# A fused block of three layers on one core: the first layer multiplies its raw input, and the RMS roots are applied behind the products

## The chip, the cores and the metric

One NeuronCore of a Trainium2 chip runs the whole program. The metric is device time in microseconds (us) from start to end of one execution; the median of three runs of the kernel before is 909.2 us (908.95 to 911.43). All data is float32; the big products run as three fp32r products of split operands. A difference of less than about 0.3% (2.7 us) can't be told from no change.

## The reference, cut to what matters

Three residual layers in a row on 256 tokens of width 1024. The change is in the first ("even") layer and in two places at the start of the second ("odd") one.

```python
def rms_norm(x, g):
    xf = x.astype(jnp.float32)
    y = xf * lax.rsqrt(jnp.mean(xf * xf, axis=-1, keepdims=True) + EPS)
    return (y * g.astype(jnp.float32)).astype(x.dtype)

def even_layer(h, mem, layer, norm_g, w_in, w_out, a_qn, a_kn, a_lam, a_on,
               b_cw, b_cb, x_qn, x_kn, mem_g, w_mem_kv):
    u = rms_norm(h, norm_g)
    proj = u @ w_in                      # 1024 -> 7168 columns
    aq, ak, av, az, bh, bc, bb, bz, xq, xz = jnp.split(proj, cuts, axis=-1)
    ya = differential_attention(aq, ak, av, a_qn, a_kn, a_lam, a_on, lam_init)   # 8 heads "A"
    yb = short_gated_conv(bh, bc, bb, b_cw, b_cb)        # bb * conv3(bc * bh)
    yx = memory_cross_attention(xq, mem, mem_g, w_mem_kv, x_qn, x_kn)            # 4 heads "X"
    y = jnp.concatenate([ya * jax.nn.silu(az), yb * jax.nn.silu(bz), yx * jax.nn.silu(xz)], axis=-1)
    return h + y @ w_out
```

The root of the first norm, 1/sqrt(mean(x^2)+eps), is one number per token. Because the product is linear, it can be multiplied onto a token's row of `proj` instead of onto `x`; where `proj` is normed again (q and k), it cancels but for the eps.

## The kernel before

**Tiling.** A weight matrix is read in *panels* of 512 columns, and a panel in four *subs* of 2 x 128 rows (512 KB each). For every sub SP loads `raw` (six slots), ScalarE (ACT) casts it into `whi`, VectorE (DVE) computes `wlo = raw - whi`, and TensorE (PE) multiplies `whi`, `wlo`, `whi` with the high, high and low part of the input. A slot of `raw` is free when `wlo` was made of it. In orientation "tok" the result has tokens on partitions (12 matmuls of 512 columns in a sub), in "col" it has features on partitions (24 matmuls of 256 columns). Results collect in two PSUM accumulators `acc` used in turn.

**Order.** `make_plan` writes one list of steps; each engine runs its share of it in that order. `pl.at(pos, ...)` hangs a step behind the sub of number `pos`. The `split` step (cast and `wlo`) of a sub is placed three subs ahead of its product (`LEAD = 3`), so DVE and ACT may run at most that far ahead, and everything else that they do stands between the splits. Subs 0 to 63 are the first layer's input panels, with the weights for the memory in between; subs 64 to 79 are `e_w_out`.

**Start.** SP loads `x` in two halves of 128 tokens, ACT squares them, GpSimd (POOL) takes the root, DVE scales the rows (L2652), PE turns them by 16 transposes (L1394, L1410), ACT and DVE take them out of PSUM as `xhi` and `xlo` in `xx` (L1766, L2658). Gains and other vectors come as rows and are turned by PE into `cols`.

**Heads.** Each head has steps qkT (transposes), scores, PT, pv; an A head also has oT: its output is scaled by its norm (L2377), turned, multiplied by gate and gain into `ytmp` (DVE L2385), cast into `yhi` (ACT L1927) and subtracted for `ylo` (DVE L2340). The panels 3072 and 3584 are the gates of the A heads, 6656 the gate of the X heads, 4096, 4608, 5120, 5632 the four inputs h, c, b, z of the convolution.

**Second layer.** The forget gate's logarithm (`forget_log`, `forget_sum`) and the first X head (head 12) stand at subs 92 to 98.

Between all this DVE also sums the modulation of the third layer out of `w_mod` (`macc`, L2403), eight halves a chunk, whose loads use the same `raw` slots.

## Time and profile before

| what | value |
|---|---|
| median of 3 runs | 909.2 us (908.95 to 911.43) |
| the profiled execution, its own time | 909.54 us |
| its span, first to last instruction | 907.7 us |
| PE busy, DVE busy, ACT busy | 887.4, 694.6, 509.6 us |
| mean granted TensorE clock | 0.998 |

How to read it: PE's matmuls are pipelined, so "busy" covers small gaps. What one costs is the distance between the starts of two in a row, and a gap shows as a larger distance and in the bracket behind a row ("[0.73 <-DVE wlo L2137]": idle 0.73 us before, released by that). An "x4" row is several merged, with the time that they span. Start times are us from the span's start. PEclk is the granted clock of a stretch (1.00 is 2.4 GHz, 0.50 is 1.2 GHz). The chain of waits is the work that ended last, followed back: each row is a piece of it.

### The profile page before, as it was taken

The page shows a single profiled execution, that of the slowest core. Times are in us where ns is not written, and L with a number is a line of the kernel's source. Part 1 is how long each engine was busy: PE and PEld are TensorE (multiplying, and loading weights), DVE is VectorE, ACT ScalarE, POOL GpSimd, SP SyncE. Part 2 cuts the span into 40 slices and gives each one's busy share as a digit, 9 for nine tenths or more (in the row PEclk, how much of TensorE's full clock was granted, in tenths as well). Part 3 has the DMA queues.
Part 4 walks back from the last instruction along what each step waited for, and adds up shares of the span by engine and source line. Part 5 has one row for each costly group of instructions (what it writes and reads, how often), then busy time and mean ns, then how long its engine had stood idle before and what let it go on. Part 6 is the DMA issues. An engine that isn't in the chain of part 4 may idle for free.

```text
span 907.7 us, 13941 instructions
## 1 busy us (share of the span) xinstructions
PE 887.4 (98%) x5136; PEld 748.0 (82%) x5136; DVE 694.6 (77%) x1094; ACT 509.6 (56%) x902; POOL 85.7 (9%) x82
## 2 busy tenths in 40 slices
PE   7999999999999999999999999999999999999997
PEld 5888878999788788988889887877787688888885
DVE  6789989879777568788898765878757779877553
ACT  6567564664445555555576646546645755555441
POOL 0302121100001101102111000100001100010000
PEclk9999999999999999999999999999999999999999
DMA  9754644736665755768767764453223468875541
GB/s 329 270 193 158 236 136 145 260 136 217 223 237 158 235 185 193 248 227 280 267 210 237 262 209 151 127 187 93 93 94 114 153 201 272 281 224 192 193 157 46
DMA packets 103125, 177.71 MB, mean 196 GB/s; under 512 B 7118, under 2 KB 32147, under 8 KB 102931
## 3 DMA queue, kind: packets, MB, share of 16 engines
q1 hardware_dynamic: 99856, 167.27, 55.1%
q0 software_dynamic: 2896, 9.42, 3.0%
q8 instruction: 42, 0.69, 0.3%
q14 instruction: 25, 0.20, 0.1%
q10 hardware_dynamic: 306, 0.14, 0.1%
HBM read 175.71 MB, written 1.07 MB: 195 GB/s over the span
## 4 chain that ended last, share of the span: by engine, by line
PE 79%; DVE 12%; ACT 4%; issue 3%; DMA 1%; POOL 1%; ACTq 0%; DVEq 0%; POOLq 0%
PE acc L1295 15%; PE acc L1297 14%; PE acc L1296 14%; PE acc L1357 9%; PE acc L1358 4%; DVE wlo L2137 4%; PE acc L1306 4%; PE acc L1307 4%; PE acc L1308 4%; ACT whi L1700 1%; DVE macc L2403 1%; PE tp L1452 1%; PE spsum L1436 1%; PE opsum L1575 1%; PE tp L1420 1%
## 5 line engine op out<-in xcount | busy, mean ns | idle before, releaser
L2137 DVE TENSOR_TENSOR wlo<-raw,whi 128x1024 fp32r<-128x1024 f32 (+2 forms) x274 | 324.6, 1193 | 101.0 <-ACT whi L1700 100.5
L1700 ACT CAST whi<-raw 128x1024 fp32r<-128x1024 f32 (+2 forms) x274 | 278.2, 1026 | 106.0 <-PE acc L1297 63.1
L1295 PE MATMUL acc<-whi,xx 128*128 128x512 f32 (+1 forms) x352 | 143.4, 408 | 1.9 <-DVE xx L2661 1.0
L1297 PE MATMUL acc<-whi,xx 128*128 128x512 f32 (+1 forms) x352 | 136.4, 388 | 0.0
L1296 PE MATMUL acc<-wlo,xx 128*128 128x512 f32 (+1 forms) x352 | 135.9, 386 | 0.0
L1357 PE MATMUL acc<-xx,whi 128*128 128x512 f32 x352 | 123.1, 394 | 0.9 <-DVE xx L2646 0.8
L1306 PE MATMUL acc<-xx,whi 128*128 128x256 f32 x384 | 112.7, 293 | 0.0
L1308 PE MATMUL acc<-xx,whi 128*128 128x256 f32 x384 | 108.6, 283 | 0.0
L1307 PE MATMUL acc<-xx,wlo 128*128 128x256 f32 x384 | 108.5, 283 | 0.0
L1358 PE MATMUL acc<-xx,wlo 128*128 128x256 f32 x352 | 98.2, 279 | 0.0
L2734 POOL TENSOR_TENSOR small<-small,half_neg 128x8 f32<-128x8 f32 (+4 forms) x30 | 50.5, 1683 | 444.8 <-DVE small L2098 269.5
L1295 PE MATMUL acc<-whi,yhi 128*128 128x512 f32 x224 | 89.2, 398 | 0.8 <-DVE wlo L2137 0.7
L1297 PE MATMUL acc<-whi,ylo 128*128 128x512 f32 x224 | 87.3, 390 | 0.0
L1296 PE MATMUL acc<-wlo,yhi 128*128 128x512 f32 x224 | 87.3, 390 | 0.0
L2403 DVE SCALAR_TENSOR_TENSOR macc<-raw,scol,macc 128x512 f32<-128x512 f32 x112 | 82.2, 755 | 0.0
L1295 PEld LDWEIGHTS acc<-whi,xx 128*128 128x128 f32 x352 | 66.5, 189 | 17.0 <-issue 5.4
L1357 PEld LDWEIGHTS acc<-xx,whi 128*128 128x128 f32 x352 | 65.9, 187 | 17.4 <-DVE xx L2646 1.4
L1297 PEld LDWEIGHTS acc<-whi,xx 128*128 128x128 f32 x352 | 66.3, 188 | 14.3
L1296 PEld LDWEIGHTS acc<-wlo,xx 128*128 128x128 f32 x352 | 66.7, 189 | 11.9
L1306 PEld LDWEIGHTS acc<-xx,whi 128*128 128x128 f32 x384 | 73.5, 191 | 1.4 <-issue 1.1
L1307 PEld LDWEIGHTS acc<-xx,wlo 128*128 128x128 f32 x384 | 73.5, 191 | 0.3
L1308 PEld LDWEIGHTS acc<-xx,whi 128*128 128x128 f32 x384 | 73.4, 191 | 0.0
(409 smaller groups left out, 1399.8 us busy)
## 6 DMA issues: line engine op xcount, KB each, us to landing
raw<-in_e_w_in SPq DMA_DIRECT2D x56, 512.0 KB, 5.6
raw<-in_o_w_in SPq DMA_DIRECT2D x56, 512.0 KB, 5.6
raw<-in_w_mod SPq DMA_DIRECT2D x48, 512.0 KB, 4.3
raw<-in_w_ffn_in SPq DMA_DIRECT2D x44, 512.0 KB, 4.9
raw<-in_w_in SPq DMA_DIRECT2D x28, 512.0 KB, 3.9
raw<-in_w_ffn_out SPq DMA_DIRECT2D x22, 512.0 KB, 4.2
raw<-in_e_w_out SPq DMA_DIRECT2D x16, 512.0 KB, 6.3
raw<-in_o_w_out SPq DMA_DIRECT2D x16, 512.0 KB, 4.9
```

Source lines behind the costliest of these rows:

```text
L1295: mm(o, hi, whi[:, slot, k, 0:pan.ncols], start=a, stop=False)
L1296: mm(o, hi, wlo[:, slot, k, 0:pan.ncols], start=False, stop=False)
L1297: last = mm(o, lo, whi[:, slot, k, 0:pan.ncols], start=False, stop=z)
L1306: mm(o, wh, hi, start=a, stop=False, skip_group_check=True)
L1307: mm(o, wl, hi, start=False, stop=False, skip_group_check=True)
L1308: return mm(o, wh, lo, start=False, stop=z, skip_group_check=True)
L1357: mm(o, wh, xx[:, kk, :, :].rearrange("p a t -> p (a t)"), start=a, stop=False)
L1358: last = mm(o[:, 0:T], wl, xx[:, kk, 0, :], start=False, stop=z)
L1700: nc.scalar.copy(slab(whi, s.i % SPLIT_SLOTS, 0, s.nk, n), slab(raw, s.raw.i % RAW_SLOTS, s.koff, s.nk, n)).then_inc(S["hi_ready"], 1)
L2137: tt(slab(wlo, slot, 0, s.nk, n), slab(raw, s.raw.i % RAW_SLOTS, s.koff, s.nk, n), slab(whi, slot, 0, s.nk, n).bitcast(F32), ALU.subtract) ...
L2403: ins = stt(m, src, c, m, ALU.mult, ALU.add)
L2734: nc.gpsimd.tensor_tensor(to, ms, half_neg[:, 0:n], ALU.pow).then_inc(S["rstd_ready"], 1)
```

## The change

1. **Start.** The host also lays out `x` turned, feature-major (`x_t`, 1 MB), and the vectors turned (`vec_cols`). SP loads weights and quarters of `x_t` in turn, and the token-major rows only after the fifth and sixth weight load. ACT and DVE make `xhi` and `xlo` straight from `x_t` (gain only, no root). The transposes, the scaling of rows and the turning of the vectors go. PE runs five matmuls on zeros first (`warm_first`).
2. **Roots behind.** The squares and the root come behind sub 2 (`fold_stat`, formerly for the memory alone). q and k use the root in their eps; v is scaled on its way out of PSUM by ACT; POOL spreads the root over all partitions as a row (`x_row`, in `negcum`). The col panels are multiplied by that row: h and b on DVE (they were ACT copies), c, z and the X gate by an extra DVE multiply in PSUM (`gate_scale`).
3. **A gates token by token.** Panels 3072 and 3584 turn from "col" to "tok". The gate is multiplied in pv_late, oT becomes one ACT and one DVE instruction.
4. **Two steps placed anew**, in the second layer: the forget logarithm is finished in `forget_log`, ahead of the next split; head 12 of the X heads starts one sub later (`first_late=1`).

```diff
@@ Plan.parts
+                    if pan.w == "e_w_in" and ev.kind in ("evac_conv_c", "evac_conv_z") or ev.kind == "evac_gate" and ev.tile == 12 and pan.w == "e_w_in":
+                        self.tick(ev, "row_scaled")
+                        self.steps.append(Step("gate_scale", first=ev))
                     self.steps.append(ev)
@@ Plan.head
-            self.tick(h.f5, "oT_ps", "ytmp_ready", "yhi_ready", "y_ready")
-            self.uses(h.f5, "tp", "ytmp_ready")
+            self.tick(h.f5, "oT_ps", "yhi_ready", "y_ready")
+            self.uses(h.f5, "tp", "y_ready")
...
-        due(0 if h.j else 1, f1, -1)
-        due(2, f2)
+        due(0 if h.j else 1 + first_late, f1, -1)
+        due(2 if h.j else 2 + first_late, f2)
@@ make_plan
-    stat = pl.row_stat(0, "g0", ("loaded_x0", 16))
-    first = pl.row_scale(stat, "g0", dve=(0, 1), act=())
-    stat = pl.row_stat(1, "g0", ("loaded_x1", 16))
-    pl.step("setup")
-    second = pl.row_scale(stat, "g0", dve=(0, 1), act=())
-    pl.step("pull")
-    pl.transposed_by_k("g0", (first, second), "x", ROW["e_norm"], None, pull=(3,))
+    pl.step("warm_first", q=5)
+    for k in range(KT):
+        if k % 2 == 0:
+            pl.step("pull")
+        pl.tick(pl.step("x_part", scale=ROW["e_norm"], q=k), "rt_hi", "rt_lo")
+    pl.src["x"] = pl.count["rt_lo"], KT
+    pl.fresh = 4
+    pl.at(2, lambda: pl.rows_stat("x", "g0", ("loaded_x0", "loaded_x1")), 1)
     pl.at(2, lambda: pl.step("load_mem_t"))
-    pl.at(0, lambda: pl.step("setup_gains"))
+    pl.at(4, lambda: pl.step("setup"), -1)
+    pl.at(4, lambda: pl.step("setup_gains"))
...
-    pl.panel(W, 3072, CW, "x", "gate", "col", tile=0)
+    pl.panel(W, 3072, CW, "x", "gate", tile=0)
...
-    b = heads("X", "g1", evs, pl.pos, 4, 12, gain="ox")
+    b = heads("X", "g1", evs, pl.pos, 4, 12, gain="ox", first_late=1)
@@ SP
-            for t in range(NT):
-                sp.dma_start(rows_of["g0"][:, t, :], w["x"][0, t * P:(t + 1) * P, :]).then_inc(S[f"loaded_x{t}"], 16)
...
+                if r.i < 4:
+                    sp.dma_start(x_t[:, 2 * r.i:2 * r.i + 2, :], w["x_t"][:, 2 * r.i * T:(2 * r.i + 2) * T].rearrange(
+                        "p (k t) -> p k t", t=T)).then_inc(S[f"loaded_xt{r.i}"], 16)
+                else:
+                    t = r.i - 4
+                    if t < NT:
+                        sp.dma_start(rows_of["g0"][:, t, :], w["x"][0, t * P:(t + 1) * P, :]).then_inc(S[f"loaded_x{t}"], 16)
@@ PE
+            def warm_first(st):
+                pe.wait_ge(S["warm_in"], 1)
+                for _ in range(st.q):
+                    mm(acc[:, 0, 0:3 * P], pbuf[:, 0:P], pbuf[:, 0:3 * P], start=True, stop=True)
@@ ACT
+            def x_part(st):
+                k = st.q
+                act.wait_ge(S["loaded_cols"], 16)
+                act.wait_ge(S[f"loaded_xt{k // 2}"], 16)
+                f(xhi[:, k, :], x_t[:, k, :], ACT.Copy, scale=scale_cols(st.scale)[:, k:k + 1]).then_inc(S["rt_hi"], 1)
...
+                if "row_scaled" in st.on:
+                    wait(("row_scaled", st.on["row_scaled"]))
                 f(gates[:, st.tile:st.tile + n, :], acct(st.acc, n), ACT.Tanh, scale=0.5).then_inc(S["tanh_ready"], 1)
...
             def oT(st):
-                wait(("ytmp_ready", st.on["ytmp_ready"]))
-                nc.scalar.copy(yhi[:, st.h.tile, :], ytmp[:, :]).then_inc(S["yhi_ready"], 1)
+                wait(("oT_ps", st.on["oT_ps"]))
+                f(yhi[:, st.h.tile, :], tp[:, 0:T], ACT.Copy, scale=gain["aon"][:, :]).then_inc(S["yhi_ready"], 1)
@@ DVE
+            def x_part(st):
+                k = st.q
+                wait(("rt_hi", st.on["rt_hi"]))
+                stt(xlo[:, k, :], x_t[:, k, :], scale_cols(st.scale)[:, k:k + 1], xhi[:, k, :].bitcast(F32), ALU.mult,
+                    ALU.subtract).then_inc(S["rt_lo"], 1)
+            def gate_scale(st):
+                ev = st.first
+                dve.wait_ge(S["sub_done"], ev.done)
+                wait(("row_in", 16))
+                z = acct(ev.acc)
+                tt(z, z, by_row(z), ALU.mult).then_inc(S["row_scaled"], 1)
+            def evac_conv_hb(st):
+                dve.wait_ge(S["sub_done"], st.done)
+                wait(("row_in", 16))
+                at = 0 if st.kind == "evac_conv_h" else 1024
+                z = acct(st.acc)
+                tt(g2[:, at:at + 1024].rearrange("p (c t) -> p c t", t=T), z, by_row(z), ALU.mult).then_inc(S["conv_ev"], 1)
@@ DVE forget_log / forget_sum
-
-            def forget_sum(st):
                 wait(("logf_e", 1))
                 stt(logf[:, :, :], fx[:, :, :], 0.0, fe[:, :, :], ALU.min, ALU.subtract).then_inc(S["logf_ready"], 1)
+
+            def forget_sum(st):
@@ DVE pv_late, oT
+                wait(("gate_ready", st.gate_ready))
+                link(tt(stat(st, 2)[:, 0:NT], stat(st, 2)[:, 0:NT], x_rstd, ALU.mult))
+                gate = gate_block(st.h.tile // 4 * 4, 4)
                 for t in range(NT):
-                    last = ts(ytok[:, t * P:(t + 1) * P], opsum[:, t * P:(t + 1) * P], stat(st, 2)[:, t:t + 1],
-                              None, ALU.mult)
+                    at = t * CW + st.h.tile % 4 * P
+                    last = stt(ytok[:, t * P:(t + 1) * P], opsum[:, t * P:(t + 1) * P], stat(st, 2)[:, t:t + 1],
+                               gate[:, at:at + P], ALU.mult, ALU.mult)
...
-                stt(ytmp[:, :], tp[:, 0:T], gain["aon"][:, :], gates[:, st.h.tile, :], ALU.mult, ALU.mult)\
-                    .then_inc(S["ytmp_ready"], 1)
-                to_lo(st, st.h.tile)
+                wait(("yhi_ready", st.on["yhi_ready"]))
+                stt(ylo[:, st.h.tile, :], tp[:, 0:T], gain["aon"][:, :], yhi[:, st.h.tile, :].bitcast(F32), ALU.mult,
+                    ALU.subtract).then_inc(S["y_ready"], 1)
@@ POOL
+            def setup(st):
+                wait(("rstd_ready", pl.fold_rstd["x"]))
+                for t in range(NT):
+                    pool.dma_start(row_scratch[t * P:(t + 1) * P, :], x_rstd[:, t:t + 1]).then_inc(S["row_out"], 16)
+                wait(("row_out", 16 * NT))
+                pool.dma_start(x_row, row_scratch.rearrange("t o -> o t").to_broadcast([P, T])).then_inc(S["row_in"], 16)
```

ACT at the start of the program, before (`g_62` holds the rows of `x`, `spsum`, `tp` and `opsum` the transposed ones):

```order
L1816 ACTIVATE scr,small<-g_62 128x1024 x2
L1700 CAST whi<-raw 128x1024
L1766 ACTIVATE xx<-spsum,cols 128x256 x2
L1766 ACTIVATE xx<-tp,cols 128x256
L1766 ACTIVATE xx<-opsum,cols 128x256
L1700 CAST whi<-raw 128x1024
```

and now (`g_63` holds `x_t`, `g_62` the rows):

```order
L1723 CAST whi<-raw 128x1024
L1778 ACTIVATE xx<-g_63,cols 128x256 x2
L1723 CAST whi<-raw 128x1024
L1778 ACTIVATE xx<-g_63,cols 128x256 x2
L1723 CAST whi<-raw 128x1024
L1778 ACTIVATE xx<-g_63,cols 128x256 x2
L1723 CAST whi<-raw 128x1024
L1778 ACTIVATE xx<-g_63,cols 128x256 x2
L1723 CAST whi<-raw 128x1024 x2
L1769 ACTIVATE scr,small<-g_62 128x1024 x2
```

The two squares moved from the first place to behind six casts.

DVE at the end of the first layer's input panels, before (`g_59` holds the convolution; the first `ytmp` is head 10's, the second head 11's):

```order
L2335 TENSOR_SCALAR pbuf<-pbuf,rinv 128x256 x2
L2351 SCALAR_TENSOR_TENSOR ytmp<-opsum,gates 128x256
L2340 TENSOR_TENSOR ylo<-ytmp,yhi 128x256
L2137 TENSOR_TENSOR wlo<-raw,whi 128x1024
...
L2403 SCALAR_TENSOR_TENSOR macc<-raw,scol,macc 128x512 x2
L2137 TENSOR_TENSOR wlo<-raw,whi 128x1024
L2217 SCALAR_TENSOR_TENSOR gates<-gates,acc 128x1024
L2351 SCALAR_TENSOR_TENSOR ytmp<-opsum,gates 128x256
L2340 TENSOR_TENSOR ylo<-ytmp,yhi 128x256
L2251 SCALAR_TENSOR_TENSOR g_59<-g_59,gates 128x1024
L2137 TENSOR_TENSOR wlo<-raw,whi 128x1024
```

and now:

```order
L2389 TENSOR_SCALAR pbuf<-pbuf,rinv 128x256 x2
L2163 TENSOR_TENSOR g_59<-acc,negcum 128x1024
L2405 SCALAR_TENSOR_TENSOR ytmp<-opsum,gates 128x256
L2394 TENSOR_TENSOR ylo<-ytmp,yhi 128x256
L2190 TENSOR_TENSOR wlo<-raw,whi 128x1024
...
L2458 SCALAR_TENSOR_TENSOR macc<-raw,scol,macc 128x512 x2
L2190 TENSOR_TENSOR wlo<-raw,whi 128x1024
L2156 TENSOR_TENSOR acc<-acc,negcum 128x1024
L2271 SCALAR_TENSOR_TENSOR gates<-gates,acc 128x1024
L2405 SCALAR_TENSOR_TENSOR ytmp<-opsum,gates 128x256
L2394 TENSOR_TENSOR ylo<-ytmp,yhi 128x256
L2305 SCALAR_TENSOR_TENSOR g_59<-g_59,gates 128x1024
```

Two multiplies by `negcum` (the row of roots) came in, the second directly ahead of the gate.

ACT in the second layer, before (`gain_ox` is the gain of the X heads; the qkT pair is head 12's):

```order
L1879 ACTIVATE g_59<-opsum 12x256
L1700 CAST whi<-raw 128x1024
L1837 ACTIVATE scr<-acc 128x1024
L1700 CAST whi<-raw 128x1024 x2
L1886 ACTIVATE qkT<-tp,gain_ox 128x256
L1887 ACTIVATE qkT<-tp 128x256
```

and now:

```order
L1910 ACTIVATE g_59<-opsum 12x256
L1723 CAST whi<-raw 128x1024
L1866 ACTIVATE scr<-acc 128x1024
L1723 CAST whi<-raw 128x1024 x3
L1917 ACTIVATE qkT<-tp,gain_ox 128x256
L1918 ACTIVATE qkT<-tp 128x256
```

Head 12's transposes moved behind one more cast, that is one sub later.

## Rows read from the trace of the kernel before

**Rows 1.** The page's first part: busy us, share of the span, instructions.
```profile
PE 887.4 (98%) x5136; PEld 748.0 (82%) x5136; DVE 694.6 (77%) x1094; ACT 509.6 (56%) x902; POOL 85.7 (9%) x82
```
**Rows 2.** Stretches: length, busy us and count by engine, PEclk, DMA share, GB/s.
```profile
13.00:20.00 7.00, 7.00 (x32) 5.75 (x31) 5.88 (x17) 4.35 (x9) 0.72 (x1) 1.00 1.06 408
171.00:190.00 19.00, 19.00 (x157) 18.02 (x155) 13.31 (x24) 12.12 (x28) 2.26 (x2) 1.00 0.55 195
203.00:231.00 28.00, 28.00 (x207) 26.83 (x206) 25.63 (x43) 13.64 (x23) 0.75 (x1) 1.00 0.62 225
904.00:907.70 3.70, 0.00 (x0) 0.00 (x0) 0.68 (x1) 0.00 (x0) 0.00 (x0) 0.50 0.38 153
```
**Rows 3.** Timeline of the start: start us, us, engine, line, op.
```profile
4.75 1.06 ACT L1816 ACTIVATE scr<-g 128x1024 f32<-128x1024 f32 x1 [1.17 <-DMA g<-in_x]
7.97 1.05 ACT L1700 CAST whi<-raw 128x1024 fp32r<-128x1024 f32 x1 [0.52 <-DMA raw<-in_e_w_in]
9.23 1.22 DVE L2137 TENSOR_TENSOR wlo<-raw,whi 128x1024 fp32r<-128x1024 f32 x1
...
11.01 0.77 PE L1295 MATMUL acc<-whi,xx 128*128 128x512 f32 x1
...
12.00 0.63 PE L1297 MATMUL acc<-whi,xx 128*128 128x512 f32 x1
12.43 0.63 PE L1295 MATMUL acc<-whi,xx 128*128 128x512 f32 x1
...
13.63 0.40 PE L1296 MATMUL acc<-wlo,xx 128*128 128x512 f32 x1
13.86 0.39 PE L1297 MATMUL acc<-whi,xx 128*128 128x512 f32 x1
```
**Rows 4.** Timeline, PE in the third layer: ten matmuls that keep it busy.
```profile
711.07 3.39 PE L1386 MATMUL acc<-cst 128*128 128x384 f32 x10
```
**Rows 5.** Timeline, PE where panel 2048 (tok) meets panel 3072 (col).
```profile
44.49 0.39 PE L1297 MATMUL acc<-whi,xx 128*128 128x512 f32 x1
44.71 0.28 PE L1306 MATMUL acc<-xx,whi 128*128 128x256 f32 x1
44.83 0.28 PE L1307 MATMUL acc<-xx,wlo 128*128 128x256 f32 x1
```
**Rows 6.** DVE groups up to 320 us: busy us, mean ns, idle before.
```profile
L2377 DVE TENSOR_SCALAR ytok<-opsum,pv_stat 128x128 f32<-128x128 f32 x16 | 4.8, 344 | 1.2 <-POOL pv_stat L2734 1.2
L2223 DVE TENSOR_TENSOR g<-g,acc 128x1024 f32<-128x1024 f32 x1 | 1.2, 1215 | 0.0
```
**Rows 7.** Timeline, DVE in the oT step of one A head.
```profile
168.47 0.47 DVE L2385 SCALAR_TENSOR_TENSOR ytmp<-tp,gain_aon,gates 128x256 f32<-128x256 f32 x1
169.41 0.42 DVE L2340 TENSOR_TENSOR ylo<-ytmp,yhi 128x256 fp32r<-128x256 f32 x1 [0.47 <-ACT yhi L1927]
```
**Rows 8.** Chain of waits at the first layer's end: start us, us, what.
```profile
222.04 3.83 DMA raw<-in_e_w_out
...
226.97 0.99 DVE wlo L2137
...
228.11 1.21 DVE gates L2217
...
233.75 1.24 DVE wlo L2137
...
235.13 0.47 PE acc L1295
```
**Rows 9.** Timeline, PE stalls: heads 8 and 12, forget sums, end.
```profile
161.28 0.41 PE L1420 MATMUL tp<-cst,g 128*128 128x128 f32 x2 [0.56 <-ACT g L1848]
...
308.54 0.39 PE L1517 MATMUL opsum<-logf,cst 128*128 128x12 f32 x2 [0.47 <-DVE logf L2283]
...
320.08 0.41 PE L1420 MATMUL tp<-cst,g 128*128 128x128 f32 x2 [0.88 <-DVE g L2209]
...
901.12 0.39 PE L1297 MATMUL acc<-whi,zlo 128*128 128x512 f32 x1
```

More of the change, by code:

```diff
@@ L467, in row_scale, with head @@
         return done
-    def head(self, h, pos, gap=4):
+    def head(self, h, pos, gap=4, first_late=0):
         h.n = self.heads
@@ L721, in make_plan @@
     b = heads("A", "g1", evs, max(b, pl.pos), 4, 4)
-    pl.panel(W, 3584, CW, "x", "gate", "col", tile=4)
+    pl.panel(W, 3584, CW, "x", "gate", tile=4)
     evs = [pl.panel(W, 6144, CW, "x", "norm", gs=128, dst=("g0", 0), heads_first=True),
@@ L1844, in evac_copy @@
                     wait(("gate_sb", 2))
-                if st.panel.w in memory_panels:
-                    wait(("rstd_ready", pl.mem_rstd))
+                if st.panel.w in fold_of:
+                    which = fold_of[st.panel.w]
+                    wait(("rstd_ready", pl.fold_rstd[which]))
                     for t in range(NT):
-                        last = f(grp(*st.dst)[:, t * CW:t * CW + CW], acc2(st.acc)[:, t, :], ACT.Copy, scale=mem_rstd[:, t:t + 1])
+                        last = f(grp(*st.dst)[:, t * CW:t * CW + CW], acc2(st.acc)[:, t, :], ACT.Copy,
+                                 scale=folds[which][1][:, t:t + 1])
                     last.then_inc(S["v_evac"], 1)
```

137 lines of the change are left out of this document (72 added, 65 removed).

## The prediction

> **What bounds the kernel now.** Read the page's first part first: PE is busy 98% of the span, DVE 77% [rows 1]. That asks for the second question, where PE waits at all, since only three things can shorten this program: a stretch in which PE has nothing, fewer or cheaper matmuls, and the few stalls. The timeline of the start gives the first. The first product starts at 11.01 us, and the distance between two 512-column products is 0.43 us there (12.00 to 12.43) and 0.23 us a little later (13.63 to 13.86) [rows 3]: PE ran at 1.2 GHz for the first 2 us of unbroken work, then at 2.4 GHz, which cost 1.0 us. So the steady stream begins, in effect, at 12.0. After that the timeline of PE shows only single stalls up to the second layer's heads: 0.56 us at head 8, 0.47 us before the forget sums, 0.88 us at head 12 [rows 9], and one at the end of the first layer's input, where the chain of waits leaves PE altogether: from 222.04 to 235.13 it goes load, cast, `wlo`, gate, `wlo` [rows 8]. There DVE is the engine that decides: in 203 to 231 it is busy 25.6 of 28.0 us [rows 2], and most of the rest is ACT's answer to its own result. The chain's 222.04 is also DVE's: a slot of `raw` came free only when DVE had read it.
>
> **The start.** Before, `x` had to arrive (the first 512 KB are there at 4.75), be squared, scaled, turned and split, and the first weights came third in the queue (cast at 7.97) [rows 3]. Now the weights are first, so their cast starts near 4.75 and ends at 5.80; `wlo` takes 1.22, to 7.0 [rows 3]; the first `xlo` (128x256 on DVE, 0.42 to 0.47 [rows 7]) ends at 7.5. The quarter of `x_t` behind the weights needs 256 KB at 408 GB/s [rows 2], 0.65 us, so it is there at 5.4 and its cast on ACT lies beside `wlo`. First product at 7.6. Per sub PE takes 12 x 0.227 = 2.72 us, DVE 1.22 + 2 x 0.45 = 2.1, ACT less, a load of 768 KB 1.9: the first four subs hold PE's pace.
>
> The clock: five matmuls of 384 columns have a distance of 0.32 us at 2.4 GHz (3.39 us for ten [rows 4]), so twice that at 1.2: 3.2 us, from about 1.1 (my estimate: DVE has to write the zeros first) to 4.3. Then PE pauses until 7.6. No row shows a pause like that with work behind it. Ends: full rate from the first product (the stream begins at 7.6, gain 12.0 - 7.6 = 4.4), or slow until the 13.0 at which the clock rose before (5.4 us at half rate, 2.7 lost, gain 1.7). I take what rows 3 show of unbroken work, 2 us slow and 1.0 lost: gain 3.4.
>
> Rows 3 show half-rate products at first though transposes had kept PE busy ahead of them. The Trainium skill (TensorE: Matmul & The Clock Gate, Part 1: The HAM clock gate) has it that the slow phase is a budget of time and not of matmuls, and that its length differs from run to run; by that alone the five matmuls would have used it up and the gain would be 4.4.
>
> Loads: the squares stand behind sub 2 and the sixth cast, and they need both halves of the rows, so ACT waits there. Until the seventh weight block must be there PE has taken six, at 7.6 + 6 x 2.72 = 23.9, or 1 us later with the slow clock. Before it come six blocks, `x_t`, the rows, the constants and, on POOL's queue, the turned memory: 3.1 + 1.0 + 1.0 + 0.5 + 1.0 + 0.5 for itself = 7.2 MB, 17.7 us at 408 GB/s from about 3.2 (4.75 less one block and the landing), so 21; cast and `wlo` make it 23.3, plus ACT's own lateness. Just in time: I put 0.5 us, bounds 0 and 2.6 (the one more MB that the start loads now). Start in sum: -2.9 (bounds -4.4 and +0.9).
>
> **A gates token by token.** A col sub is 24 matmuls at 0.12, 2.88 us; a tok sub 12 at 0.227, 2.72 [rows 5]. Eight subs: -1.3, all on PE's path. Bounds -1.0 to -1.6 for the rounding of the rows.
>
> **oT of A heads.** DVE had 0.47, then 0.47 idle for ACT, then the second instruction (rows 7: 168.47 to 169.83). Now ACT goes first, from PSUM, and DVE does one instruction: -0.9 us of DVE a head. pv_late gains a tiny instruction and reads the gate beside (its 128x128 instructions cost 0.34 now [rows 6]): +0.35. So -0.5 us of DVE for each of 8 heads. PE doesn't wait for DVE there except at head 8 (0.56), which I count as gone: -0.6. Bounds 0 and -0.6. `tp` is now held until both have read it; the next user of `tp` stands a sub later, 2.7 us, which covers it.
>
> **Scaling by the row of roots.** Five instructions of 128x1024 come to DVE, on the X gate, h, c, b, z; the nearest row, one that also reads `acc`, has 1.22 [rows 6]; the next instruction starts 1.14 behind the start of one of this size (226.97 to 228.11 [rows 8]), so each takes 1.13 of DVE's time. Two ACT copies go, but ACT isn't what is waited for. The X gate and h come at 172 and 185: DVE has 19.0 - 13.31 = 5.7 us free in 171 to 190 [rows 2], more than the two take with a tanh between them, and PE has no stall there: hidden. c (at 199) and b (at 217) stand in the full stretch of rows 2; I let 0.3 of the two go into gaps: +1.9 at the chain's 222.04. z is the worst: at 228.11 the gate's instruction [rows 8] now waits for `gate_scale` (1.13) and then for ACT's tanh, which can't start before it (1.0): +2.1. Everything behind it is in series: convolution product, cast, `wlo`, PE at 235.13. Sum +4.0. Bounds: 0 if the waits in that chain take all of it, +6.8 if all five (5.7) and a tanh (1.1) come through. I take 4.0 since the chain has no gap over 0.5 us before 230.
>
> **Second layer.** With the logarithm ahead of the next `wlo`, which waits for ACT's cast anyway, the 0.47 goes; with head 12 a sub (2.7 us) later its 0.88 goes [rows 9]. The scores follow at the old distance, and PT's place stays, still three subs on. -1.4, bounds 0 and -1.5.
>
> **Sum.** -2.9 - 1.3 - 0.6 + 4.0 - 1.4 = -2.2. The profiled execution took 909.5, 0.3 above the median: 907.3, or 907.0 against the median runs. I say 907.1.
>
> **Rivals.** *The scaling hides* (for it: DVE is lighter by 4 us through the A heads, and in rows 8 it waits 3.83 us for a load whose issue may come from another slot; against it: PE is never more than three subs behind DVE, so lightness before 190 isn't carried on). Then only z's 2.1 counts, and with the clock up from the start: 907.1 - 1.9 - 1.0 = 904.2.
> *The start is bound by its loads* (for: 408 GB/s is all that the queues gave in 13 to 20; against: the arithmetic above leaves room). The 2.6 us of the additional MB come through instead of 0.5: 909.2, no change.
> *The clock falls in the two pauses* (slower). PE would pause 3.3 us after the five matmuls, and the stall before 235.13 grows from 0.9 to about 5 in one piece, where before no pause inside the program reached 2. For it: PE's last matmul starts at 901.12 [rows 9], and 904.0 to 907.7 has a granted clock of 0.50 [rows 2]: under 3 us of idleness were enough. Each fall costs up to the 5.4 us from 7.6 to 13.0 at half rate, 2.7. The first is 1.7 more than I counted, the second 2.7: 907.1 + 4.4 = 911.5. It decides from a pause of some 3 us on; against it: the pauses may come out shorter, and work resumes at once. The Trainium skill (same page, HAM oscillation) describes such a fall over a wait for data in every round of a loop; the end of this trace agrees with it.
> *The change doesn't do what it says*: the gates could still be bound elsewhere. In the order of instructions 16 transposes and 96 matmuls are gone from PE, so I give that nothing.
>
> **How the numbers follow.** Forecast 0.42 (its own range 905.3 to 908.9), hidden scaling 0.28, load-bound start 0.13, clock 0.17. The range reaches from 903.2 to 911.5, a little past the second case and to the fourth. What a measurement of this kernel can tell from no change is 0.3%, 2.7 us, so faster means under 906.5: all of hidden scaling and a third of the forecast, 0.42; slower means over 911.9: less than half of the clock case and what I overlooked, 0.14; same 0.44.
>
> **What would show it.** First product near 7.6, distance 0.43 for about 2 us: the start; a PE gap between 20 and 27 us released by a cast that waited for a load: the second rival. PE about 4 us earlier at sub 12 (44.71 before), 5 at the last A gate. At head 8 no stall. Before the fourth sub of `e_w_out` (235.13) a stall of 4 to 5 us with DVE `gates` behind ACT's tanh in its chain; if it is 2 or less, the scaling was hidden. Distances of 0.43 behind that stall or behind the first product for more than 3 us: the clock. No gap over 0.3 us at the forget sums and head 12. Wrong altogether would be a stall that I don't name, of `tp` in A heads above all.

## The result: 4.0 us slower, and the profile after

The changed kernel takes 914.9 us (median of 5 runs, 914.5 to 915.6), the kernel before took 911.0 us in runs beside it (5 runs, 909.0 to 912.0). The ratio is 1.0048, interval 1.0035 to 1.0060: slower. I had forecast 907.1 us.

Where it went is read by laying the start of each sub's product on PE beside the same start before. Where the difference changes, the change gained or lost. "Product 12" is the product of sub 12 here and in the expectations; minus is sooner than before.

| products | difference behind them | what happened |
|---|---|---|
| 0, 1 | -4.06 | start of the stream, full clock |
| 6, 8, 12 | +0.93 at 13 | three stalls: +1.25, +1.75, +1.70, and +0.31 in small steps |
| 13 to 33 | -0.21 at 33 | A gates token by token: eight steps of -0.02 to -0.16, -0.85 in all; -0.30 at 33 |
| 46, 47 | -1.21 at 60 | head 8's stall and one behind it gone: -0.75, -0.26 |
| 63, 67, 68 | +5.27 at 80 | +0.69, +3.66, +2.09 (half clock) |
| 95 to 101 | +3.49 at 101 | second layer: -0.73, -1.42, -0.39, then +0.57, +0.19 |
| 200 to 260 | +5.40 at 260 | third layer, which the change doesn't touch |

Of the last row a reader should know this: a kernel that differs from before only in its first 7 us (below) also lost 2.05 us between products 200 and 260, and another nothing. The profiled execution before seems to be one without that loss; it is 1.4 us under its median, so the spans differ by 5.8 us and the medians by 4.0.

The page's first part of the changed kernel, answering to [rows 1], hardly moves:

```profile
PE 890.6 (97%) x5032; PEld 743.4 (81%) x5032; DVE 697.5 (76%) x1096; ACT 510.7 (56%) x904; POOL 86.0 (9%) x84
```

104 records fewer on PE and yet more busy time: the ten records of the warm-up are 6.53 us by themselves (PE was busy 4.33 us before the first product of before), and matmuls at half clock last longer. The timeline of PE up to 60 us, of which I show the first product and every row with idle time before it (start us, us, engine, line, op; in brackets the idle time and its releaser):

```profile
1.32 6.53 PE L1404 MATMUL acc<-pbuf 128*128 128x384 f32 x10 [1.32 <-DVE pbuf L2143]
7.88 0.47 PE L1316 MATMUL acc<-whi,xx 128*128 128x512 f32 x1
...
25.64 0.47 PE L1316 MATMUL acc<-whi,xx 128*128 128x512 f32 x1 [1.09 <-DVE wlo L2190]
32.95 0.50 PE L1316 MATMUL acc<-whi,xx 128*128 128x512 f32 x1 [1.59 <-DVE g L2262]
45.67 0.50 PE L1316 MATMUL acc<-whi,xx 128*128 128x512 f32 x1 [1.54 <-DVE g L2262]
```

The start is as good as hoped: 7.88 against 11.01 [rows 3]. Three stalls take it back; before, this stretch had none. The first waits for `wlo`, whose cast (ACT, 23.19) waited for its load; the other two wait for DVE to take a q or k panel out of `acc`, which needs that panel's root from POOL. So the next view is POOL's timeline there:

```profile
11.53 0.70 POOL L2832 DMA_DIRECT2D h_res<-in_mem_t  x1 [10.68 <-PE acc L1318]
22.65 0.73 POOL L2789 TENSOR_TENSOR lam_x<-small,half_neg 128x2 f32<-128x2 f32 x1 [10.42 <-DVE small L2128]
26.91 3.83 POOL L2789 TENSOR_TENSOR small<-small,half_neg 128x16 f32<-128x16 f32 x1 [3.54 <-DVE small L2255]
30.70 1.16 POOL L2826 DMA_DIRECT2D row_scratch<-lam_x  x2
40.86 0.55 POOL L2828 DMA_DIRECT2D negcum<-row_scratch  x1 [9.00 <-DMA row_scratch<-lam_x]
41.42 2.93 POOL L2789 TENSOR_TENSOR small<-small,half_neg 128x16 f32<-128x16 f32 x1
```

The row of roots is written to memory at 30.70 and fetched again at 40.86. Between the two POOL stands still for 9.00 us, and the next panel's root (41.42) is queued behind the fetch.

The first layer's end, timeline of DVE, then of ACT (one fence each), answering to [rows 8]:

```profile
228.86 1.23 DVE L2156 TENSOR_TENSOR acc<-acc,negcum 128x1024 f32<-128x1024 f32 x1
231.24 1.22 DVE L2271 SCALAR_TENSOR_TENSOR gates<-gates,acc 128x1024 f32<-128x1024 f32 x1 [1.15 <-ACT gates L1896]
...
233.61 1.22 DVE L2305 SCALAR_TENSOR_TENSOR g<-g,gates 128x1024 f32<-128x1024 f32 x1
236.88 1.23 DVE L2190 TENSOR_TENSOR wlo<-raw,whi 128x1024 fp32r<-128x1024 f32 x1 [2.06 <-ACT whi L1723]
```
```profile
230.18 1.03 ACT L1896 ACTIVATE gates<-acc 128x1024 f32<-128x1024 f32 x1 [2.49 <-DVE acc L2156]
...
234.86 1.04 ACT L1900 CAST yhi<-g 128x1024 fp32r<-128x1024 f32 x1 [1.62 <-DVE g L2305]
235.81 3.89 ACT L1723 CAST whi<-raw 128x1024 fp32r<-128x1024 f32 x4
```

DVE's gate (228.11 before) is at 231.24: 1.13 for the scaling, 1.15 for the tanh that now waits for it, the rest, 0.85, is lateness that it brings along from earlier. Read on to what PE waits for: the `wlo` of 236.88, from the cast at 235.81. That cast's weights had long arrived (four casts run in one go), but it stands in ACT's order behind the copy of the convolution's result. PE has nothing for 4.39 us, and then the clock goes. Stretches of the changed kernel (length, busy us and count by engine, PEclk, DMA share, GB/s), answering to [rows 2]:

```profile
229.00:236.00 7.00, 4.86 (x22) 3.70 (x20) 4.20 (x5) 2.57 (x4) 0.00 (x0) 1.00 0.36 136
236.20:243.00 6.80, 4.75 (x11) 3.80 (x12) 6.12 (x7) 3.50 (x4) 0.00 (x0) 0.50 0.21 44
243.00:250.00 7.00, 7.00 (x37) 5.17 (x36) 3.88 (x5) 2.60 (x4) 0.60 (x1) 1.00 1.03 373
```

### The profile page after: what moved, and what is told of

It reads as the page before. It is cut to its first block, busy times and chain, and to the rows that moved or that the text cites. A ratio compares the mean times of both kernels' runs of the same rounds, so it can differ in the third digit from the quotient of the medians.

```text
span 913.5 us, 13756 instructions
## 1 busy us (share of the span) xinstructions
PE 890.6 (97%) x5032; PEld 743.4 (81%) x5032; DVE 697.5 (76%) x1096; ACT 510.7 (56%) x904; POOL 86.0 (9%) x84
## 4 chain that ended last, share of the span: by engine, by line
PE 79%; DVE 8%; DMA 4%; ACT 3%; issue 3%; POOL 1%; SPq 1%; ACTq 0%; DVEq 0%
PE acc L1316 16%; PE acc L1318 15%; PE acc L1317 15%; PE acc L1378 7%; PE acc L1379 4%; PE acc L1327 3%; PE acc L1328 3%; PE acc L1329 3%; DVE wlo L2190 2%; DMA raw<-in_e_w_in 1%; POOL small L2789 1%; ACT whi L1723 1%; DMA row_scratch<-lam_x 1%; PE tp L1476 1%; PE spsum L1460 1%
## 5 line engine op out<-in xcount | busy, mean ns | idle before, releaser
L1316 PE MATMUL acc<-whi,xx 128*128 128x512 f32 (+1 forms) x384 | 156.5, 407 | 6.3 <-DVE g L2262 3.1
L1318 PE MATMUL acc<-whi,xx 128*128 128x512 f32 (+1 forms) x384 | 148.8, 387 | 0.0
L1317 PE MATMUL acc<-wlo,xx 128*128 128x512 f32 (+1 forms) x384 | 148.0, 385 | 0.0
L1379 PE MATMUL acc<-xx,wlo 128*128 128x256 f32 x352 | 98.5, 280 | 0.0
L1327 PE MATMUL acc<-xx,whi 128*128 128x256 f32 x320 | 94.0, 294 | 0.4 <-DVE wlo L2190 0.4
L1316 PEld LDWEIGHTS acc<-whi,xx 128*128 128x128 f32 x384 | 72.2, 188 | 24.7 <-issue 7.2
L1329 PE MATMUL acc<-xx,whi 128*128 128x256 f32 x320 | 90.5, 283 | 0.0
L1328 PE MATMUL acc<-xx,wlo 128*128 128x256 f32 x320 | 90.4, 283 | 0.0
L2789 POOL TENSOR_TENSOR small<-small,half_neg 128x8 f32<-128x8 f32 (+4 forms) x28 | 48.5, 1733 | 427.9 <-DVE small L2128 244.6
L1318 PEld LDWEIGHTS acc<-whi,xx 128*128 128x128 f32 x384 | 72.1, 188 | 15.6
L1317 PEld LDWEIGHTS acc<-wlo,xx 128*128 128x128 f32 x384 | 72.4, 189 | 12.9
L1378 PEld LDWEIGHTS acc<-xx,whi 128*128 128x128 f32 x352 | 65.9, 187 | 19.0 <-DVE gates L2725 1.5
L1379 PEld LDWEIGHTS acc<-xx,wlo 128*128 128x128 f32 x352 | 66.5, 189 | 0.0
L1327 PEld LDWEIGHTS acc<-xx,whi 128*128 128x128 f32 x320 | 61.2, 191 | 1.7 <-issue 1.4
L1328 PEld LDWEIGHTS acc<-xx,wlo 128*128 128x128 f32 x320 | 61.2, 191 | 0.2
```

Source lines behind the costliest of these rows:

```text
L1316: mm(o, hi, whi[:, slot, k, 0:pan.ncols], start=a, stop=False)
L1317: mm(o, hi, wlo[:, slot, k, 0:pan.ncols], start=False, stop=False)
L1318: last = mm(o, lo, whi[:, slot, k, 0:pan.ncols], start=False, stop=z)
L1327: mm(o, wh, hi, start=a, stop=False, skip_group_check=True)
L1328: mm(o, wl, hi, start=False, stop=False, skip_group_check=True)
L1329: return mm(o, wh, lo, start=False, stop=z, skip_group_check=True)
```

## The experiments

Theory after the result: three causes besides the extra work. (1) POOL's round trip of the row stalls product 12, and the early 1 MB load stalls 6 and 8. (2) The scaling lengthens the sequence on ACT and DVE that the weights' split is queued behind. (3) The stall of (2) lets the clock fall. The main rival to (2): VectorE is full in 203 to 231, so it counts how much work is added, not where it stands.

Before measured 910.7 to 911.2 us beside the later runs. Where a kernel has a ratio, both sides have 5 runs or more and its 95% interval is about 0.1% to either side. A single time can be 1 to 2 us off, so the kernels with one run are judged by their steps. All differences in the table are those of one profiled execution against that of before, in us, at the product named; the last column is how long the granted clock was 0.50 inside the program.

| kernel | time | at 13 | at 60 | at 80 | at 101 | half clock lasted |
|---|---|---|---|---|---|---|
| changed | 914.9 | +0.93 | -1.21 | +5.27 | +3.49 | 6.83 |
| row's fetch apart | 911.7 (1 run) | -0.80 | -2.95 | +2.66 | +0.87 | 3.41 |
| mem load later | 913.6 (1 run) | -1.71 | -3.83 | +3.62 | +1.83 | 6.83 |
| z not scaled | 910.1 (1 run) | -0.27 | -2.39 | +1.00 | -0.78 | 3.41 |
| nothing scaled | 907.5 (1 run) | -0.31 | -2.43 | -2.48 | -4.26 | 0 |
| PE busy in the pause | 911.6 (1 run) | +0.62 | -1.52 | +2.86 | +1.08 | 0 |
| b last | 913.5 | +0.32 | -1.82 | +3.35 | +1.57 | 6.83 |
| b last, start mended | 909.4 | -3.15 | -5.27 | -0.09 | -1.87 | 6.83 |
| late end | 909.7 | +0.55 | -1.57 | -0.16 | -1.94 | 0 |
| all mended | 906.1 | -3.21 | -5.35 | -4.33 | -6.11 | 0 |
| result sooner | 907.5 | -3.34 | -5.59 | -3.57 | -5.35 | 0 |
| before, warm | 910.5 | -0.85 | -0.79 | -0.87 | -0.85 | 0 |
| before, two steps | 908.7 | -0.81 | -0.52 | -0.68 | -2.33 | 0 |

### The row's fetch parted from its write

```diff
+    pl.at(8, lambda: pl.step("row_out"), 5)
+    pl.at(13, lambda: pl.step("row_in"), 5)
     # setup(POOL) split: row_out writes the two halves, row_in waits for them and fetches
```

> The changed kernel, with POOL's spreading of the root cut in two steps that stand later: the write of the roots behind sub 8, the read of the row behind sub 13, so that POOL waits for no write ahead of a root. Theory (POOL's wait of 9.3 us for its own write holds the root of panel 1024, whose accumulator sub 12 wants): the stall of 1.7 us before sub 12 is gone, sub 12 starts at 44.0 instead of 45.7. Rival (the loads and DVE are next in line and as late): under 0.5 us is won, and the stall stays at sub 12 or moves to one of the next subs.

Measured 911.66 us in one run. The step at product 12 is 0.00 instead of 1.70, those at 6 and 8 stay (1.13, 1.75), so does 3.66 at 67. In the POOL rows of this kernel the root of the next panel (36.68) stands ahead of the write. POOL still waits for the write before its fetch, 6.48 us up to 48.84, but nothing that a product needs is queued behind:

```profile
36.68 3.81 POOL L2791 TENSOR_TENSOR small<-small,half_neg 128x16 f32<-128x16 f32 x1 [5.84 <-DVE small L2257]
40.45 1.17 POOL L2828 DMA_DIRECT2D row_scratch<-lam_x  x2
...
48.84 0.57 POOL L2832 DMA_DIRECT2D negcum<-row_scratch  x1 [6.48 <-DMA row_scratch<-lam_x]
```

What it shows: the stall at 12 is POOL's place in the order, not the root itself. In the kernels that keep the round trip there this stall was 1.70, 1.20, 1.11, 1.00, 0.70, 0.47 and 0.35; in the three later ones that part it too it is gone as well.

### mem transposed loaded behind the root of x

```diff
-    pl.at(2, lambda: pl.step("load_mem_t"))
+    pl.at(2, lambda: pl.step("load_mem_t"), 2)
```

> The changed kernel with one edit: GpSimd issues the 1 MB load of mem transposed behind the root of x, not ahead of it. In the run with both mends the step at product 6 (1.25 us) was gone and that at 8 was 0.72 instead of 1.75. Theory (the load beside the weights made products 6 and 8 wait): here too the step at 6 goes and that at 8 is 0.6 to 0.9, while the stall at product 12 stays (0.4 to 1.7, by when the row's write lands); profile 1.8 to 2.5 us earlier from product 9 on. Rival (parting the row's write from its fetch did it): steps of 1.25 and 1.75 as in the changed kernel.

As the theory had it: 0.00 at product 6, 0.88 at 8, 1.20 at 12. A PE row (product 8) and POOL rows of this kernel:

```profile
30.77 0.50 PE L1316 MATMUL acc<-whi,xx 128*128 128x512 f32 x1 [0.72 <-DVE g L2262]
```
```profile
20.84 0.70 POOL L2789 TENSOR_TENSOR lam_x<-small,half_neg 128x2 f32<-128x2 f32 x1 [19.99 <-DVE small L2128]
21.50 0.71 POOL L2832 DMA_DIRECT2D h_res<-in_mem_t  x1
24.74 3.85 POOL L2789 TENSOR_TENSOR small<-small,half_neg 128x16 f32<-128x16 f32 x1 [2.54 <-DVE small L2255]
```

The root of `x` comes at 20.84 instead of 22.65 and the first panel's at 24.74 instead of 26.91: the load beside had delayed the rows of `x` and the weights alike. Of 3.0 us lost at products 6 and 8, 2.1 were this load. What is left at 8 (0.9) is the sequence of root, panel root (3.85 us of POOL) and evacuation. In the three later kernels with both mends the step at 6 is gone too and that at 8 is 0.56 to 0.72. Of the 2.6 us won at product 13 here only 1.7 were left at 80: the stall before product 67 was longer in this execution (4.74 us, steps of 4.01 and 2.73).

### z not scaled, and nothing scaled

```diff
-  if pan.w == "e_w_in" and ev.kind in ("evac_conv_c", "evac_conv_z") or ...:
+  if pan.w == "e_w_in" and ev.kind in ("evac_conv_c",) or ...:      # z left as it is
+  if False:                                                          # second kernel: X gate, c, z; h and b copied by ACT
```

> The changed kernel without the multiply by the row of roots on the z panel of the convolution (left out: the gate z isn't normalised). Theory (the multiply and the tanh behind it stand in series ahead of sub 67): 2.1 to 2.3 us less of the 4.6 us stall before sub 67, and with a pause of only some 2.4 us the clock doesn't fall behind it, another 2.1 us: sub 68 starts 4.2 us earlier. Rival (DVE is late by the earlier scalings anyway): under 1 us less.

> The changed kernel without any of the five multiplies by the row of roots (left out: the X gate and all four convolution inputs aren't normalised; h and b are copied by ACT as in the kernel before). Theory (these five are the whole loss at the end of the first layer): the stalls before subs 63 and 67 are 0 and at most 0.9 us as in the kernel before, the clock doesn't fall, and the step of 6.4 us that the changed kernel shows between subs 62 and 68 against the kernel before is gone. Rival (the changed gates or the shifted loads hold part of it): 1 us or more of the step stays.

Both kernels leave a part of the computation out and serve only to price it. Measured 910.14 and 907.52 us. Without z's scaling the step at 67 is 1.25 instead of 3.66: 2.41 for one instruction of 1.13 and a tanh that waits. Without any, the steps at 63, 67 and 68 are 0.00, -0.07 and 0.00. One PE row of each, with the stall (1.99, 0.66):

```profile
234.64 0.47 PE L1316 MATMUL acc<-whi,yhi 128*128 128x512 f32 x1 [1.99 <-DVE wlo L2190]
```
```profile
232.62 0.47 PE L1316 MATMUL acc<-whi,yhi 128*128 128x512 f32 x1 [0.66 <-DVE wlo L2188]
```

So the whole 6.4 us of this place are the row scaling, its size as in my sum (4.35 of them), plus the clock. Half of the first expectation missed: the clock fell even with 1.99 us of stall, at 235.70, when work had been going again for 1.1 us, and the step at 68 was still 1.45. How long the low stretch lasted varied (3.41 and 6.83).

### PE kept busy in the pause

```diff
+    pl.at(pl.pos + 2, lambda: pl.step("warm_z", q=7, c=ev.acc, waits=[("gate_ready", ev.on["gate_ready"])]), 3)
```

> The changed kernel with seven idle matmuls of 384 columns (4.5 us) on PE behind sub 66, in the pause before sub 67. Theory (the clock fell in that pause, and the matmuls behind it ran at half rate for 6.8 us, of which PE worked 4.7): the stall stays, but the distance of products behind it is 0.23 and sub 68 starts 2.0 us earlier. Rival (the longer distance comes from operands or PSUM, not from the clock): no difference at sub 68.

The step at 67 stays (3.68), the one at 68 is 0.00 instead of 2.09. The PE row of the idle matmuls and the stretch that answers to the half-clock one:

```profile
233.39 4.68 PE L1411 MATMUL acc<-cst 128*128 128x384 f32 x14
```
```profile
236.20:243.00 6.80, 6.78 (x32) 4.33 (x31) 6.41 (x7) 3.21 (x4) 0.00 (x0) 1.00 0.21 69
```

The clock's fall is a consequence of the pause and costs 2.1 us by itself. This takes nothing off the cause of the pause.

### Before, with warm matmuls alone; before, with the two steps alone

```diff
+    pl.step("warm_first", q=4)          # before + four 384-column matmuls ahead of its transposes
```

> The kernel before with nothing but four full-width matmuls put ahead of its first transposes (1.3 to 6.5 us, two records of 0.64 us each). It shows what of the 4.06 us won at the start is the clock alone. In the kernel before the first product ran from 11.01 to 13.0 us at half clock (five matmuls at 0.43 us apart instead of 0.23) and the transposes before it too. Theory (most of the gain is the missing normalisation and transposes): first product at 10.5 to 11.0, second product 1.0 to 1.5 us earlier, time 909.7. Rival (the clock made the gain): 3 us or more earlier, 907.5 or less.

910.5 us, ratio 0.9999 (0.9990 to 1.0008). The second product came 0.84 sooner, and the theory's 1.0 seems met. But the kernel with the two steps alone, whose start is that of before to the letter, shows 0.85 as well. Their PE rows (warm, then two steps):

```profile
1.32 5.18 PE L1386 MATMUL acc<-pbuf 128*128 128x384 f32 x8 [1.32 <-DVE pbuf L2115]
...
11.10 0.47 PE L1296 MATMUL acc<-whi,xx 128*128 128x512 f32 x1 [0.63 <-DVE xx L2667]
11.40 0.40 PE L1297 MATMUL acc<-wlo,xx 128*128 128x512 f32 x1
```
```profile
11.09 0.47 PE L1295 MATMUL acc<-whi,xx 128*128 128x512 f32 x1 [0.36 <-DVE xx L2658]
11.39 0.40 PE L1296 MATMUL acc<-wlo,xx 128*128 128x512 f32 x1
```

In [rows 3] the clock rose at 13.0 us, in this other execution of the same start at 10.1. So a part of the 4.06 that looked won at the start, 0.9, is how the clock fell out in one execution of before, and warming alone is worth nothing that can be measured. What is sure is the first product, 7.9 against 11.0.

```diff
-        due(2, f2)
+        due(2 if h.j else 2 + first_late, f2)      # forget_sum's logarithm moved into forget_log too
```

> The kernel before with only the two steps placed anew in the second layer: the log of the forget gates finished a step earlier on VectorE, and the first head's scores one product later. In the changed kernel the second layer's products 95 to 99 came 2.54 us sooner against before and 0.76 of it was lost again right behind. Theory (these two edits do that alone): a net step of -1.78 between products 94 and 104, nothing before it; time 911.0 - 1.8 = 909.2. Rival (a part of it came from the changed layer in front, whose late end moved the loads of the second layer): a step of -1 or less, 910 or more.

908.7 us, ratio 0.9978 (0.9969 to 0.9987). Between products 94 and 101 the difference goes from -0.55 to -2.33: -1.78, as the changed kernel had it there to the hundredth. The rival is out.

### b last

The convolution's panels in the order h, c, z, b. ACT copies h out, POOL multiplies it twice by the row, later also the gates; `b` is multiplied straight from PSUM.

```diff
-    pl.panel(W, 5120, CW, "x", "conv_b", "col")
-    ev = pl.panel(W, 5632, CW, "x", "conv_z", "col", tile=8)
+    pl.panel(W, 5632, CW, "x", "conv_z", "col", tile=8)
+    ev = pl.panel(W, 5120, CW, "x", "conv_b", "col")
+    nc.gpsimd.tensor_tensor(a, a, by_row(a), ALU.mult)      # h twice, gates once
```

> The changed kernel, with the convolution panels in the order h, c, z, b. ScalarE copies h out unscaled and GpSimd, which is idle there, multiplies it twice by the row of roots (the root of h and that of c); z is scaled, sent through tanh and multiplied into the convolution while b runs; GpSimd multiplies the gates of z once more (the root of b); b is multiplied straight from PSUM as the last step. VectorE so loses three of its four 1.2 us row multiplications, and the chain behind the last product of the panels loses scaling, tanh and a gate product. Theory (what the layer's end costs is the length of the chain behind its last panel, 3.66 us at product 67 and 0.69 at product 63, and the 2.09 us of half clock are its consequence): the step at product 67 becomes zero or negative against the kernel before (down to -2), the clock does not fall at 236 us, and the time is 914.9 - 6 = 909 (907.5 to 910.5). Rival (VectorE's busy time before the layer's end is what costs, and each row multiplication the same wherever it stands): three of four go, 914.9 - 3 = 912. Rival (GpSimd beside VectorE slows VectorE's wlo by more than is saved): slower than 914.9.

> The same as the run with b last, and the two places of the start mended too: the fetch of the spread row stands five places behind its write (as in the run that parted them), and the load of mem transposed is issued behind the root of x, so that the weights of the first products have the DMA engines for longer. Theory: the row's stall at product 12 (1.70 us) goes wholly; of the 1.25 and 1.75 us at products 6 and 8 at least the first goes, if it is the 1 MB load beside the weights that made them late; 909 - 1.7 - (0 to 3.0) = 906 (904.5 to 908), faster than both kernels. Rival (the weights are late whatever stands beside them, since all of x, its transpose and the weights must come): the steps at 6 and 8 stay at 3.0 together and the time is 907.3. Rival (later mem loads stall the memory's parts instead): a new step near products 9 to 14 of up to 3 us, 909 to 910.

Both missed: 913.5 us (1.0029, 1.0018 to 1.0039) and 909.4 (0.9988, 0.9978 to 0.9999). The step at 67 was gone (-0.90), as the theory said, and two others had come: 3.91 at product 63 and 2.33 at 64, the clock again. Why is in DVE's, ACT's, POOL's and PE's rows of "b last":

```profile
216.69 1.23 DVE L2160 TENSOR_TENSOR acc<-acc,negcum 128x1024 f32<-128x1024 f32 x1
219.07 1.22 DVE L2268 SCALAR_TENSOR_TENSOR gates<-gates,acc 128x1024 f32<-128x1024 f32 x1 [1.15 <-ACT gates L1896]
...
221.10 1.92 DVE L2391 TENSOR_TENSOR ylo<-ytmp,yhi 128x256 fp32r<-128x256 f32 x1 [0.47 <-ACT yhi L1958]
222.94 1.21 DVE L2187 TENSOR_TENSOR wlo<-raw,whi 128x1024 fp32r<-128x1024 f32 x1
```
```profile
218.01 1.03 ACT L1896 ACTIVATE gates<-acc 128x1024 f32<-128x1024 f32 x1 [4.94 <-DVE acc L2160]
```
```profile
220.39 2.35 POOL L2838 TENSOR_TENSOR gates<-gates,negcum 128x1024 f32<-128x1024 f32 x1 [10.63 <-DVE gates L2268]
```
```profile
224.30 0.55 PE L1327 MATMUL acc<-xx,whi 128*128 128x256 f32 x1 [3.66 <-DVE wlo L2187]
```

Three of DVE's row multiplications were gone, and the place cost 5.17 us between products 60 and 80 against 6.48. The sequence scaling, tanh, gate had only moved a panel forward, with the next split still queued behind all of it; ACT stood 4.94 us before its tanh. A part of the third rival is in the rows too: the `ylo` of 221.10 took 1.92 us instead of 0.42 while POOL's product of 220.39 ran, so 1.5 of the 3.91 us are POOL's. The order gave the last theory. The mends of the start worked in the second kernel: 0.00, 0.72 and 0.00 at products 6, 8, 12.

### The same work, its end written between the splits

```diff
-    st = pl.step("conv", gate=ev.on["gate_ready"])       # and evac_conv_z at the panel's end
+    pl.at(pl.pos + 0, lambda: pl.step("gate_scale", first=ev), 1)
+    pl.at(pl.pos + 0, lambda: pl.step("conv_tanh", first=ev), 2)
+    pl.at(pl.pos + 1, lambda: pl.steps.append(ev), 1)     # gate product on DVE
+    pl.at(pl.pos + 2, conv, 2)
```

> The changed kernel with the end of the convolution written later: the scaling of z and its tanh one product behind their panel, the gate product two and the convolution's last product three, each with the split of a weight slab between. The 1.2 us row multiplications are all still there. The tiles that come of it are first multiplied by product 70. Theory (PE waits at product 67 for weights whose split stands in ScalarE's and VectorE's order behind scaling, tanh, gate product and copy, and not for the convolution itself; the fall of the clock is that wait's consequence): the steps at 67 (3.66) and 68 (2.09) go, 0.69 at product 63 stays, and the time is 914.9 - 5.75 = 909.2 (908.5 to 910.5). Rival (VectorE has no time left before the layer's end, and 4.9 us more work costs its own length wherever it stands): 3 to 4 us of loss turn up elsewhere between products 60 and 72, 912.5 or more. Rival (the convolution's result is now late): a stall at product 70 of 1 to 3 us, 910.5 to 912.

909.7 us, ratio 0.9983 (0.9974 to 0.9992). This is the changed kernel with all its added work and only the order altered: 5.2 us faster than it, and faster than before. The steps at 67 and 68 went from +3.66 and +2.09 to -0.90 and -0.21. A part of the second rival came true: +1.67 at product 70, which waits for the result itself. DVE and PE rows:

```profile
231.53 1.23 DVE L2165 TENSOR_TENSOR acc<-acc,negcum 128x1024 f32<-128x1024 f32 x1
...
235.99 1.21 DVE L2280 SCALAR_TENSOR_TENSOR gates<-gates,acc 128x1024 f32<-128x1024 f32 x1
237.12 1.22 DVE L2199 TENSOR_TENSOR wlo<-raw,whi 128x1024 fp32r<-128x1024 f32 x1
238.25 1.22 DVE L2314 SCALAR_TENSOR_TENSOR g<-g,gates 128x1024 f32<-128x1024 f32 x1
```
```profile
243.96 0.50 PE L1325 MATMUL acc<-whi,yhi 128*128 128x512 f32 x1 [1.51 <-DVE ylo L2319]
```

DVE no longer waits for the tanh itself: a split stands between each two links. The rival of a full VectorE wanted 3 to 4 us to turn up elsewhere and 912.5 us; between products 60 and 80 the difference grew by 1.41, and 0.90 of stall that before had at product 67 is gone in that sum.

### All mended, and the result one product sooner

The late end, POOL's two products for h, and both mends of the start; then the same with

```diff
-    pl.at(pl.pos + 2, conv, 2)
+    pl.at(pl.pos + 1, conv, 2)
```

> The same late end of the convolution, and besides: h copied out by ScalarE and multiplied twice by the row of roots on GpSimd (two of the four row multiplications so leave VectorE), the row's fetch parted from its write, and mem transposed loaded behind the root of x. Theory: the start keeps 3.15 us to product 13 as in the run with both mends, 5.3 at product 60; the convolution costs 0 to 0.7; with -1.8 of the second layer the products behind it stand 6.4 to 7.1 us before those of the kernel before, and the time is 910.7 - 6.7 + 1 (what the third layer's loads have taken in most runs) = 905 (903.5 to 906.5), ratio about 0.994, faster than both. Rival (VectorE full before the layer's end): 2 to 3 us more, 907.5 to 908. Rival (GpSimd beside VectorE holds VectorE up, as when a 128x256 row of VectorE took 1.9 us instead of 0.4 beside GpSimd's 2.35 us product): new steps near product 54, 906 to 907.

> The kernel with all mended (906.1), the last product of the convolution one product sooner, right behind the gate product. There product 70 waited 1.51 us more for the convolution's result than for its weights. Theory: result and copy come about 2.4 us sooner, the step of 1.56 at product 70 goes to 0 to 0.4, and the weights of product 68 or 69 do not come late: 906.1 - 1.3 = 904.8. Rival (the split of weights is now queued behind the copy again, as in the changed kernel): a step of 1 to 2 us at product 68 or 69, 906 or more.

All mended: 906.1 us, ratio 0.9944 (0.9931 to 0.9958), inside the expected range and the fastest, 8.8 us under the changed kernel. With the result sooner 907.5 (0.9965, 0.9952 to 0.9977): the rival was right. Product 70 no longer waits (0.12), but product 69 does (2.40), for a `wlo` whose cast is again behind the copy:

```profile
233.18 1.23 DVE L2320 SCALAR_TENSOR_TENSOR g<-g,gates 128x1024 f32<-128x1024 f32 x1
236.47 1.22 DVE L2205 TENSOR_TENSOR wlo<-raw,whi 128x1024 fp32r<-128x1024 f32 x1 [2.06 <-ACT whi L1734]
```
```profile
237.84 0.47 PE L1327 MATMUL acc<-whi,yhi 128*128 128x512 f32 x1 [2.19 <-DVE wlo L2205]
```

## Why the prediction was wrong, step by step

**First product: right.** 7.6 forecast, 7.88 measured. **The warm-up: mis-sized.** I counted 3.2 us and a pause. The ten records of L1386 [rows 4] come from five instructions: a float32 matmul of 384 columns leaves two records. So the five here ran from 1.32 to 7.85 with no pause, and the clock was up at 7.48. The gain read 4.06 against 3.4 forecast (4.4 was the upper bound), 0.9 of it belonging to the one execution compared with.

**The loads and roots at the start: this step failed.** I put 0.5 us, bounds 0 and 2.6, and looked for one stall, that of a late weight. It came, in the named window (25.64), and cost 1.25. But I had costed the new POOL work at nothing: the step `setup`, moved there, issues two writes and a fetch that waits for them, and behind it stands the root of the next panel. Together with the root of the first panel, late by the same load, that was 1.75 and 1.70 more: 4.7 us in place of 0.5. The start's sum was -2.9 (bounds -4.4 and +0.9), measured +0.93 at product 13. Parting the fetch took 1.70 away and moving the load 2.1; with both the difference at product 13 was -3.15 to -3.34, which shows the two causes.

**A gates: mis-sized.** -1.3 forecast with bounds -1.0 to -1.6, -0.85 measured over the eight subs (-0.98 to -1.02 in the kernels without the stall at product 12); only two of the eight steps reached the -0.16 that I counted for each. **Head 8: right**, -0.75 where 0.6 was forecast; -0.26 and -0.30 more at products 47 and 33, unnamed. **`tp`**: no stall.

**Row scaling: size right, reason half right.** +4.0 forecast, 0.69 + 3.66 = 4.35 measured, and its parts fit too: z 2.1 forecast and 2.41 measured, c and b 1.9 forecast and 1.91 left without z (0.66 + 1.25). I argued with VectorE's busy share in 203 to 231. The runs put most of it elsewhere: with the same work and another order 1.41 of 6.48 us is left. What was scarce was a gap between two splits, not VectorE. The X gate and h were hidden, as forecast: from product 13 to 60 the difference moves by -2.1 with them and without.

**The clock: a rival, at 0.17, came half true.** +2.09 at product 68 (I gave 2.7, from a pause of some 3 us on); the pause after the warm-up was not there in the profiled execution. In "b last", "b last, start mended" and "result sooner", which start alike, the clock rose earlier (4.3 to 4.7 us), PE paused 1.43 to 1.67 us before the first product, and the clock stayed up. From the forecast -2.2 to +3.49 at product 101 are 5.7 us; the start's 3.8 and the clock's 2.1 are all of it, and the other misses cancel. Another 1.9 came in the third layer, which no term of mine had.

**Second layer: close.** -1.78 against -1.4 (bounds 0 and -1.5); both places alone gave the same -1.78.

**The rivals.** "The scaling hides" is out (2.41 for z alone). "Bound by its loads" was the nearest for the start, at 2.6, but its mechanism was one of two. The chance of 0.14 for slower was too low: two independent rivals that both cost had been weighed apart and never added.

## What to carry to other kernels

When work is moved into an in-order queue, cost what is queued behind it, not only what it does: a DMA round trip of 1 KB held POOL for 9 us, and with the write behind the root and the fetch five products later it cost nothing. When an engine alternates between feeding the bottleneck (here the splits) and a serial sequence with another engine (scale, tanh, gate, copy), write one feeding step between each two links; the same instructions in that order were worth 5.2 us. The last link can be too late as well as too early, and one product either way is to be measured: 906.1 against 907.5.
